# Query and key projections spread among the steps of neighbourhood attention, and its output accumulated in two PSUM banks instead of four

## The chip, the cores and the metric

The kernel runs on one core of a Trainium2 chip. A core has a matrix engine (TensorE, PE in the rows), a vector engine (VectorE, DVE), a scalar engine (ScalarE, ACT), GpSimd (POOL) and a sync engine (SyncE, SP), which issues nearly all transfers here. Each engine takes its instructions strictly in the order of its own program and waits on semaphores that the others raise. The metric is device time in microseconds for one execution, lower is better. Before the change three runs gave 3113.78, 3114.00 and 3114.54 us.

## What is computed

Two transformer blocks stand one behind the other, all in float32. The change lies in the second one, in its layer of neighbourhood attention: 512 tokens on a grid of 8 rows and 64 columns, 16 heads of 64, and 256 further context tokens to which every query attends. Cut to what matters:

```
q, k, v = jnp.split(a_lat @ w_qkv, 3, axis=-1)
qc, kc, vc = ... jnp.split(a_ctx @ w_qkv, 3, axis=-1)
s_lat = einsum('bnqhd,brnkhd->bhnqrk', q * scale, kb) + bias      # band of keys around the query
s_lat = where(col_ok, s_lat, NEG_INF)
s_ctx = einsum('bnqhd,bchd->bhnqc', qr, kc)
p = softmax(concatenate([s_lat, s_ctx], -1), -1)
o = einsum('bhnqrk,brnkhd->bnqhd', p_lat, vb) + einsum('bhnqc,bchd->bnqhd', p_ctx, vc)
o_lat @ w_out
```

Every large projection is made of three fp32r matmuls a product (`products`: high weights by low data, low weights by high data, high by high), whose sum stands in for one float32 product.

## The kernel before

`schedule()` writes one list of work items, and each engine's program walks that list and executes the items that concern it. So the place of an item in the list sets the order of its work on every engine at once, and an engine that must wait inside an item holds back all of its later items. Waits are only those on data and on buffers that must be free.

Weights come in blocks of 128 by 1024. SyncE loads them into a ring of three raw buffers (`NR`), ScalarE casts each into a high part (L1439, `t_whi`), and VectorE (even blocks, L1730) or GpSimd (odd blocks, L2157) subtracts to make the low part `t_wlo`. There are four slots for finished blocks (`NH`); `over` puts the `prep` item of block j+4 right behind the last matmul of block j. SyncE may load a block only when both parts of the block three before it are made.

`neighbourhood()` works in two halves of eight heads; a half has four pairs of heads (c) and each pair four blocks of 128 queries (b), 16 steps p = 4c + b. First the value rows of the half are made (`rows`, `rows_by_group`), SyncE copies shifted versions of them within the chip's memory (`na_shift`, L1151 and L1153, six transfers), the bias strips of the pair are loaded (`na_strip`, L1159, two transfers) and GpSimd subtracts them from the masks (`na_bias`, L2202, two instructions for each of three tables y). For one step the work goes

- `na_scores`: PE L1380 into banks 0 and 1 (one a head), drained by VectorE L2100, which adds the bias table of that kind of block and takes the row extremes; ScalarE L1680 exponentiates. Scores of p+1 need both banks drained.
- `na_probs` (one step later): VectorE L2108 and L2110 (TENSOR_SCALAR) scale the weights.
- `na_turn` (two steps later): PE L1391 transposes into banks 2 and 3, ScalarE L1686 copies out.
- `na_attend` (three steps later): PE L1407 multiplies with the values, into banks 4 and 5 for even pairs and 6 and 7 for odd ones.
- `na_y`: when a pair's four blocks are done, ScalarE L1693 and VectorE L2115 split its output into a high and a low part, head 0 at step 4c+7 and head 1 at step 4c+8.

Queries (`na_q`, 24 matmuls of 512 columns) and keys (`na_k`, 24 of 512 and 24 of 256) of pair c are projected by `q_and_k(c)` ahead of the scores of step p = c, so in the first four steps of each half. Steps 4 to 15 hold attention alone. Behind step 15 of half 0 the value rows of half 1 stand (two groups at steps 16 and 17, four after the last attend); behind step 15 of half 1 stands the output projection (`o_steps`, first in banks 0 and 1, then `na_o` on VectorE L2125).

Of the kernel before, what the change touches and what calls it, by code (L numbers as in the profile page):

```python
# [8 lines left out]
ALU = mybir.AluOpType  # L9
# [120 lines left out]
def schedule():  # L130
# [651 lines left out]
    def neighbourhood():  # L782
        pro = state["misc_free"]
        ov = {"q": pro, "k": pro, "v": pro}
        vslot = lambda tt: tt if tt < 4 else tt + 3
# [10 lines left out]
        o_specs = [(("na_o", j), (SLOT,), DC, ("yn",), [(0, "drain_dve", o_post(j))]) for j in range(DC)]  # L796
        o_steps = by_steps(o_specs[:4], SUB1, (0, 1))

# [5 lines left out]
        for half in range(2):  # L804
# [16 lines left out]

            def q_post(g, c, half=half):
                put("na_q", half=half, c=c, g=g.id, bank=g.bank, after=ov["q"])

            def k_post(g, c, half=half):
                put("na_k", half=half, c=c, g=g.id, bank=g.bank, t0=g.t0, n=g.n, after=ov["k"])

            def q_and_k(c, half=half):
                columns([(("na_qk", half * 4 + c), (SLOT,), DC, ("h", 6),
                          [(0, "drain_act", lambda g: q_post(g, c))])], SEG1, banks=(6, 7))  # L830
                last_h = columns([(("na_qk", 8 + half * 4 + c), (SLOT,), DC, ("h", 6),
                                   [(0, "drain_act", lambda g: k_post(g, c))])], SEG2, banks=(6, 7))
                state["h_free"] = [last_h]

# [28 lines left out]
            def attend(p, half=half):  # L863
                c, b = divmod(p, 4)
                to = [p % 2 * 2 + hd for hd in range(2)]
                banks = [4 + c % 2 * 2 + hd for hd in range(2)]
                before = [seat(banks[hd], "drain_dve", ("na_yh", half, c, hd)) if b == 0 else [] for hd in range(2)]
                put("na_attend", half=half, p=p, c=c, b=b, to=to, banks=banks, before=before,
                    tiles=(VSTART[BAND0[b]], VSTART[BAND0[b] + 128], 7, 8))
                for k in to:  # L870
                    turned_free[k] = [("na_ps", ("o", half, p))]

            strips(0)
            for y in range(3):
                bias(0, y)
            for p in range(16 + 3):
                if p < 4:
                    q_and_k(p)
                if p < 16:
                    c, b = divmod(p, 4)  # L880
                    scores(p)
# [12 lines left out]
                if p == 16 and half == 1:  # L894
                    closing()
                if p in (16, 17) and half == 0:
                    next(v_rows)
                if p >= 16 and half == 1:
                    next(o_steps), next(o_steps)
                if 0 <= p - 2 < 16:  # L900
                    turn_weights(p - 2)
                if p - 3 >= 0:
                    attend(p - 3)
                    for hd in range(2):
                        c, b = divmod(p - 4 - hd, 4)
# [262 lines left out]
def tensor_program(e, w, S, m, items):  # L1168
# [225 lines left out]
    def na_attend(it):  # L1394
# [4 lines left out]
        for kt in range(4):  # L1399
# [5 lines left out]
            for hd in range(2):  # L1405
                v = NVV + t * 512 + (it.c * 2 + hd) * 64
                done = e.matmul(m.PS[hd * 64:hd * 64 + 64, it.banks[hd], it.b * P:(it.b + 1) * P], m.at(v, 64),  # L1407
                                m.na_t(it.to[hd])[:, kt // 2, kt % 2 * P:(kt % 2 + 1) * P], start=kt == 0, stop=kt == 3,
# [13 lines left out]
def scalar_program(e, w, S, m, items, release):  # L1422
# [288 lines left out]
def vector_program(e, w, S, m, items, release):  # L1711
# [400 lines left out]
    def na_y(it):  # L2112
        k, pp = it.half * 4 + it.c, slice(it.hd * 64, it.hd * 64 + 64)
        w.wait_ge("na_act", ("y", k, it.hd))
        e.tensor_tensor(m.hid(1, k, 512, 0, L)[pp, :], m.PS[pp, it.bank, :], m.hid(0, k, 512, 0, L)[pp, :], ALU.subtract).then_inc(  # L2115
            *S["drain_dve"].of(("na_yh", it.half, it.c, it.hd), *([("na_y", it.half, it.c)] if it.hd else [])))

# [246 lines left out]
```

## Time and profile before

| what | value |
| --- | --- |
| median of three runs | 3114.0 us |
| the profiled execution | 3116.97 us |
| its span | 3115.2 us |
| PE busy | 2932.8 us, 94% of the span |
| PE weight loads (PEld) | 2476.5 us, 79% |
| DVE busy | 1508.3 us, 48% |
| ACT busy | 1049.0 us, 34% |
| POOL busy | 617.0 us, 20% |
| mean granted TensorE clock | 0.973 of full speed |

The profiled execution took 1.8 us more than its span, which counts from the first instruction to the last. A matmul's record outlasts the slot in which it is issued, so start-to-start distances tell what PE needs, and "idle" in a row understates a wait by a little.

### The profile page before, as it was taken

The numbers are of one execution on the slowest core, as the hardware profiler recorded it, in microseconds if no ns is written. First come the engines' busy times: TensorE is split into PE (matmuls) and PEld (weight loads), VectorE is DVE, ScalarE is ACT, GpSimd is POOL, SyncE is SP. The second block draws the span as 40 slices with busy tenths as digits, with TensorE's granted clock in tenths as the row PEclk, the third lists the DMA queues.
The fourth block names the chain that finished last, engine by engine and source line by source line (L and its number), as shares of the span: only waits on it lengthen the run. The fifth ranks groups of instructions, "written<-read, shape, count | busy, mean of one in ns | idle before, by whom it ended". The sixth has DMA issues, their size and how long they took to land.

```text
span 3115.2 us, 39771 instructions
## 1 busy us (share of the span) xinstructions
PE 2932.8 (94%) x15968; PEld 2476.5 (79%) x15968; DVE 1508.3 (48%) x2524; ACT 1049.0 (34%) x1814; POOL 617.0 (20%) x330
## 2 busy tenths in 40 slices
PE   7999977889999899999999799999998999899997
PEld 6888965678878886868687788888896777878887
DVE  4667575555766424233232835445555526532224
ACT  4322335543232532122222541122226535342222
POOL 2333212113323110101011011111102212112221
PEclk9999998889999999999999999999998999999999
DMA  3444321014444220102011023223312121122221
GB/s 136 166 147 164 115 76 54 27 55 163 151 155 141 76 75 34 61 14 82 27 68 41 28 67 124 88 82 122 115 55 88 57 68 45 55 76 100 96 100 55
DMA packets 84696, 268.80 MB, mean 86 GB/s; under 512 B 8992, under 2 KB 16544, under 8 KB 84128
## 3 DMA queue, kind: packets, MB, share of 16 engines
q1 hardware_dynamic: 84512, 266.25, 25.2%
q8 instruction: 127, 2.08, 0.3%
q14 instruction: 57, 0.47, 0.0%
HBM read 262.54 MB, written 2.10 MB: 85 GB/s over the span
## 4 chain that ended last, share of the span: by engine, by line
PE 82%; DVE 9%; ACT 5%; issue 2%; POOL 1%; DMA 1%; SPq 0%; DVEq 0%; ACTq 0%; POOLq 0%
PE ps L1170 25%; PE ps L1171 24%; PE ps L1172 24%; PE ps L1357 3%; PE ps L1348 1%; DVE t_misc L1820 1%; ACT t_whi L1439 1%; DVE t_misc L1750 1%; DVE t_wlo L1730 1%; PE ps L1380 1%; PE ps L1407 1%; POOL t_wlo L2157 1%; PE ps L1391 1%; PE ps L1260 1%; DVE t_x L1772 0%
## 5 line engine op out<-in xcount | busy, mean ns | idle before, releaser
L1170 PE MATMUL ps<-t_h,t_whi 128*128 128x512 f32 (+1 forms) x2736 | 975.5, 357 | 57.4 <-DVE t_wlo L1730 30.1
L1171 PE MATMUL ps<-t_h,t_wlo 128*128 128x512 f32 (+1 forms) x2736 | 968.2, 354 | 0.0
L1172 PE MATMUL ps<-t_h,t_whi 128*128 128x512 f32 (+1 forms) x2736 | 967.1, 353 | 0.0
L2157 POOL TENSOR_TENSOR t_wlo<-t_raw,t_whi 128x1024 fp32r<-128x1024 f32 (+3 forms) x201 | 485.9, 2417 | 2038.5 <-ACT t_whi L1439 2038.5
L1170 PEld LDWEIGHTS ps<-t_h,t_whi 128*128 128x128 f32 x2736 | 525.8, 192 | 133.1 <-issue 23.1
L1171 PEld LDWEIGHTS ps<-t_h,t_wlo 128*128 128x128 f32 x2736 | 526.0, 192 | 69.2 <-issue 1.0
L1172 PEld LDWEIGHTS ps<-t_h,t_whi 128*128 128x128 f32 x2736 | 525.1, 192 | 69.4
L1730 DVE TENSOR_TENSOR t_wlo<-t_raw,t_whi 128x1024 fp32r<-128x1024 f32 (+3 forms) x201 | 252.6, 1257 | 672.3 <-ACT t_whi L1439 672.0
L1170 PE MATMUL ps<-t_hid,t_whi 128*128 128x256 f32 (+1 forms) x1648 | 535.2, 325 | 16.8 <-DVE t_hid L1862 8.9
L1439 ACT CAST t_whi<-t_raw 128x1024 fp32r<-128x1024 f32 (+3 forms) x402 | 402.2, 1002 | 401.6 <-PE ps L1172 378.0
L1171 PE MATMUL ps<-t_hid,t_wlo 128*128 128x256 f32 (+1 forms) x1648 | 531.1, 322 | 0.0
L1172 PE MATMUL ps<-t_hid,t_whi 128*128 128x256 f32 (+1 forms) x1648 | 530.3, 322 | 0.0
L1170 PEld LDWEIGHTS ps<-t_hid,t_whi 128*128 128x128 f32 x1648 | 316.8, 192 | 44.4 <-DVE t_hid L1862 9.5
L1171 PEld LDWEIGHTS ps<-t_hid,t_wlo 128*128 128x128 f32 x1648 | 317.0, 192 | 23.0 <-issue 0.2
L1172 PEld LDWEIGHTS ps<-t_hid,t_whi 128*128 128x128 f32 x1648 | 316.6, 192 | 23.0
L1820 DVE CUSTOM_DVE_ANT_0 t_misc<-t_raw,t_misc 128x1024 f32<-128x1024 f32 x192 | 322.1, 1714 | 23.9 <-ACT t_misc L1431 16.5
L1515 ACT CAST t_hid<-t_tmp 128x512 fp32r<-128x512 f32 (+1 forms) x118 | 65.1, 552 | 381.8 <-DVE t_tmp L1859 381.8
L1859 DVE TENSOR_TENSOR t_tmp<-t_misc,ps 128x512 f32<-128x512 f32 (+1 forms) x118 | 70.6, 599 | 144.4 <-PE ps L1172 124.8
L1878 DVE SCALAR_TENSOR_TENSOR t_x<-ps,t_mod,t_x 128x256 f32<-128x256 f32 (+1 forms) x160 | 89.7, 574 | 78.1 <-PE ps L1172 78.0
L1170 PE MATMUL ps<-t_wlo,t_h 128*128 128x512 f32 x288 | 118.1, 410 | 6.3 <-DVE t_h L1811 3.1
L1862 DVE TENSOR_TENSOR t_hid<-t_tmp,t_hid 128x512 fp32r<-128x512 f32 (+1 forms) x118 | 84.9, 720 | 73.0 <-ACT t_hid L1515 73.0
L1171 PE MATMUL ps<-t_whi,t_h 128*128 128x512 f32 x288 | 114.9, 399 | 0.0
(225 smaller groups left out, 2467.0 us busy)
## 6 DMA issues: line engine op xcount, KB each, us to landing
t_raw<-in_gu SPq DMA_DIRECT2D x176, 512.0 KB, 3.2
t_raw<-in_ada SPq DMA_DIRECT2D x96, 512.0 KB, 3.3
t_raw<-in_dn SPq DMA_DIRECT2D x48, 448.0 KB, 3.3
t_raw<-in_dn SPq DMA_DIRECT2D x28, 512.0 KB, 3.6
t_raw<-in_ret_v SPq DMA_DIRECT2D x16, 512.0 KB, 3.2
t_raw<-in_ret_qk SPq DMA_DIRECT2D x16, 512.0 KB, 3.2
t_raw<-in_ret_g SPq DMA_DIRECT2D x16, 512.0 KB, 3.2
t_raw<-in_ret_o SPq DMA_DIRECT2D x16, 512.0 KB, 3.6
```

The source lines that it names most:

```text
L1170: e.matmul(out, whi, xlo, start=first, stop=False, skip_group_check=shared)
L1171: e.matmul(out, wlo, xhi, start=False, stop=False, skip_group_check=shared)
L1172: return e.matmul(out, whi, xhi, start=False, stop=last, skip_group_check=shared)
L1357: done = e.matmul(m.PS[:, c, 0:it.n], m.at(RVV + it.kt * 512 + c * P, P), pw, start=it.i == 0, stop=it.last)
L1439: e.copy(m.WHI[:, j % NH, 0:n], m.RAW[:, it.raw % NR, 0:n]).then_inc(*S["hi"].of(j))
L1515: e.copy(m.hid(0, it.k, it.pitch, it.t0, it.n), m.tmp(it.off, it.n)).then_inc(*S["hid_hi"].of(it.los[0]))
L1730: e.tensor_tensor(m.WLO[:, j % NH, 0:n], m.RAW[:, it.raw % NR, 0:n], m.WHI[:, j % NH, 0:n], ALU.subtract).then_inc(*S["lo_dve"].of(j))
L1820: e.tensor_tensor_reduce(m.at(ADA_OUT + who * 1024, 1024), m.RAW[:, it.raw % NR, :], m.cond(who), 1.0, 0.0, ALU.mult, ALU.add, m.mod(it.la ...
L1859: e.tensor_tensor(t, s, m.ps(it), ALU.mult).then_inc(*S["drain_dve"].of(it.g, ("up", it.f, *it.los[0][1:3], it.t0)))
L1862: e.tensor_tensor(m.hid(1, it.k, it.pitch, it.t0, it.n), t, m.hid(0, it.k, it.pitch, it.t0, it.n), ALU.subtract).then_inc(*S["hid_lo"].of( ...
L1878: e.scalar_tensor_tensor(out=x, in0=m.ps(it), scalar=m.mod(it.layer, it.who, it.gm, it.j), in1=x, op0=ALU.mult, op1=ALU.add).then_inc(*S[" ...
L2157: e.tensor_tensor(m.WLO[:, j % NH, 0:n], m.RAW[:, it.raw % NR, 0:n], m.WHI[:, j % NH, 0:n], ALU.subtract).then_inc(*S["lo_pool"].of(j))
```

## The change

The projections of pair n+1 (pairs counted 0 to 7 across both halves) now stand inside the attention steps of pair n: its queries at b = 1, its keys at b = 2, after that step's attend. Only pair 0 is projected ahead of its half; pair 4, the first of half 1, is projected during steps 13 and 14 of half 0, so that half 1 begins with scores. All pairs accumulate their output in banks 4 and 5. `na_y` is one item for both heads, at b = 2 of the next pair, ahead of the keys. The output projection begins at step 14 of half 1 in banks 6 and 7, with two of its steps there and one in each later step. The weight blocks are used in the new order (pair 4's ahead of the values of half 1). The arithmetic is the same. The core of the diff:

```diff
-            def q_and_k(c, half=half):
-                columns([(("na_qk", half * 4 + c), (SLOT,), DC, ("h", 6),
-                          [(0, "drain_act", lambda g: q_post(g, c))])], SEG1, banks=(6, 7))
...
+            def queries(pair):
+                half, c = divmod(pair, 4)
+                after = [("na_ps", ("s", 0, c * 4 + 3, 1))] if half else pro
...
             def attend(p, half=half):
                 c, b = divmod(p, 4)
                 to = [p % 2 * 2 + hd for hd in range(2)]
-                banks = [4 + c % 2 * 2 + hd for hd in range(2)]
-                before = [seat(banks[hd], "drain_dve", ("na_yh", half, c, hd)) if b == 0 else [] for hd in range(2)]
+                before = [seat(4 + hd, "drain_dve", ("na_yh", half, c, hd)) if b == 0 else [] for hd in range(2)]
...
+            if half == 0:
+                queries(0)
+                keys(0)
             for p in range(16 + 3):
-                if p < 4:
-                    q_and_k(p)
+                c, b = divmod(p, 4)
                 if p < 16:
-                    c, b = divmod(p, 4)
                     scores(p)
...
-                if p == 16 and half == 1:
-                    closing()
...
-                if p >= 16 and half == 1:
-                    next(o_steps), next(o_steps)
...
                 if p - 3 >= 0:
                     attend(p - 3)
-                    for hd in range(2):
-                        c, b = divmod(p - 4 - hd, 4)
-                        if 0 <= c < 3 and b == 3:
-                            put("na_y", half=half, c=c, hd=hd, bank=4 + c % 2 * 2 + hd, over=state["hid_free"])
-            for hd in range(2):
-                put("na_y", half=half, c=3, hd=hd, bank=6 + hd, over=state["hid_free"])
-            ov["q"] = ov["k"] = [("na_ps", ("s", half, 15, 1))]
+                    if b == 2:
+                        put("na_y", half=half, c=c - 1, over=state["hid_free"])
+                if p < 16 and half * 4 + c < 7:
+                    if b == 1:
+                        queries(half * 4 + c + 1)
+                    if b == 2:
+                        keys(half * 4 + c + 1)
+                elif half == 1:
+                    if p == 14:
+                        closing()
+                        next(o_steps)
+                    if p >= 14:
+                        next(o_steps)
```

The first place is PE's program at the start of half 0. Before, where L1380 is the scores of step 0 and L1170 to L1172 are the projection on either side of it:

```order
L1171 MATMUL ps<-t_h,t_wlo 128x256
L1172 MATMUL ps<-t_h,t_whi 128x256
L1380 MATMUL ps<-t_misc 128x256 x4
L1170 MATMUL ps<-t_h,t_whi 128x512
L1171 MATMUL ps<-t_h,t_wlo 128x512
```

Now, with every line number one higher:

```order
L1172 MATMUL ps<-t_h,t_wlo 128x256
L1173 MATMUL ps<-t_h,t_whi 128x256
L1381 MATMUL ps<-t_misc 128x256 x8
L1171 MATMUL ps<-t_h,t_whi 128x512
L1172 MATMUL ps<-t_h,t_wlo 128x512
```

The scores of steps 0 and 1 now stand directly one behind the other, with no projection between them.

The second place is ScalarE's program in half 0 around steps 6 to 9. Before (L1680 the exponential of a step, L1686 the copy of turned weights, L1693 the high part of the pair's output):

```order
L1686 COPY t_x<-ps 128x2x256 x2
L1680 ACTIVATE t_tmp,t_misc<-t_tmp,t_misc 128x512 x2
L1686 COPY t_x<-ps 128x2x256 x2
L1693 CAST t_hid<-ps 64x512
L1680 ACTIVATE t_misc<-t_misc 128x512 x2
L1686 COPY t_x<-ps 128x2x256 x2
L1693 CAST t_hid<-ps 64x512
```

Now (L1669 copies the next pair's queries, L1674 its keys, L1440 casts a weight block, L1696 is the high part of the output):

```order
L1687 COPY t_x<-ps 128x2x256 x2
L1669 ACTIVATE t_misc<-ps 128x512
L1440 CAST t_whi<-t_raw 128x1024
L1681 ACTIVATE t_tmp,t_misc<-t_tmp,t_misc 128x512 x2
L1687 COPY t_x<-ps 128x2x256 x2
L1696 CAST t_hid<-ps 64x512 x2
L1674 COPY t_misc<-ps 128x512
```

The two casts of the pair's output have moved together and stand in the step whose end is the projection of keys.

The third place is ScalarE's program between the halves. Before (L1526 copies value rows, L1668 the queries and L1673 the keys of pair 4):

```order
L1693 CAST t_hid<-ps 64x512 x2
L1526 COPY t_misc<-ps 128x512 x5
L1439 CAST t_whi<-t_raw 128x1024 x4
L1526 COPY t_misc<-ps 128x512
L1668 ACTIVATE t_misc<-ps 128x512
L1439 CAST t_whi<-t_raw 128x1024
L1673 COPY t_misc<-ps 128x512
L1673 COPY t_misc<-ps 128x256
L1439 CAST t_whi<-t_raw 128x1024
L1680 ACTIVATE t_misc<-t_misc 128x512 x2
```

Now:

```order
L1696 CAST t_hid<-ps 64x512 x2
L1527 COPY t_misc<-ps 128x512 x5
L1440 CAST t_whi<-t_raw 128x1024 x4
L1527 COPY t_misc<-ps 128x512
L1681 ACTIVATE t_misc<-t_misc 128x512 x2
L1681 ACTIVATE t_tmp,t_misc<-t_tmp,t_misc 128x512 x2
L1669 ACTIVATE t_misc<-ps 128x512
```

Pair 4's queries and keys are gone from between the last copy of value rows and the first exponentials of half 1. The order of SyncE's transfers up to the strips of pair 4 is the same as before.

## Rows read from the trace of the kernel before

**Rows 1.** The page: busy time of each engine, chain that ended last.

```profile
PE 2932.8 (94%) x15968; PEld 2476.5 (79%) x15968; DVE 1508.3 (48%) x2524; ACT 1049.0 (34%) x1814; POOL 617.0 (20%) x330
...
PE 82%; DVE 9%; ACT 5%; issue 2%; POOL 1%; DMA 1%; SPq 0%; DVEq 0%; ACTq 0%; POOLq 0%
```

**Rows 2.** Timeline of PE, scores: start, duration, line, [idle before, releaser].

```profile
2455.50 1.13 PE L1380 MATMUL ps<-t_misc 64*128 64x256 f32 x8
...
2465.43 1.14 PE L1380 MATMUL ps<-t_misc 64*128 64x256 f32 x8
...
2468.55 1.14 PE L1380 MATMUL ps<-t_misc 64*128 64x256 f32 x8
...
2471.66 1.13 PE L1380 MATMUL ps<-t_misc 64*128 64x256 f32 x8
...
2480.05 1.13 PE L1380 MATMUL ps<-t_misc 64*128 64x256 f32 x8 [1.03 <-DVE t_misc L2100]
...
2498.79 1.13 PE L1380 MATMUL ps<-t_misc 64*128 64x256 f32 x8
...
2602.75 1.13 PE L1380 MATMUL ps<-t_misc 64*128 64x256 f32 x8
...
2646.05 1.13 PE L1380 MATMUL ps<-t_misc 64*128 64x256 f32 x8
```

**Rows 3.** Timeline of ACT and DVE behind step 8's scores (2471.66).

```profile
2472.82 0.58 ACT L1693 CAST t_hid<-ps 64x512 fp32r<-64x512 f32 x1
2473.43 0.68 DVE L2115 TENSOR_TENSOR t_hid<-ps,t_hid 64x512 fp32r<-64x512 f32 x1 [0.64 <-ACT t_hid L1693]
...
2474.04 0.67 DVE L2100 CUSTOM_DVE_ANT_1 t_tmp<-ps,t_misc 128x512 f32<-128x512 f32 x1
```

**Rows 4.** Timeline of POOL and DVE behind the last keys of half 0.

```profile
2457.07 2.37 POOL L2157 TENSOR_TENSOR t_wlo<-t_raw,t_whi 128x1024 fp32r<-128x1024 f32 x1 [13.46 <-ACT t_whi L1439]
...
2458.09 1.63 DVE L2110 TENSOR_SCALAR t_tmp<-t_tmp,t_misc 128x512 f32<-128x512 f32 x1
```

**Rows 5.** Timeline of the first scores of half 0 and their drains.

```profile
2409.51 1.13 PE L1380 MATMUL ps<-t_misc 64*128 64x256 f32 x8 [0.56 <-ACT t_misc L1673]
2410.57 0.50 PE L1170 MATMUL ps<-t_h,t_whi 128*128 128x512 f32 x1
...
2411.26 0.69 DVE L2100 CUSTOM_DVE_ANT_1 t_misc<-ps,t_misc 128x512 f32<-128x512 f32 x1
```

**Rows 6.** Timeline between the halves, PE, SP and POOL.

```profile
2542.07 0.39 PE L1172 MATMUL ps<-t_whi,t_h 128*128 128x512 f32 x1
2542.30 0.39 PE L1170 MATMUL ps<-t_h,t_whi 128*128 128x512 f32 x1
...
2548.73 1.07 SPq L1159 DMA_DIRECT2D t_misc<-in_rpb  x2
...
2555.05 4.20 POOL L2202 TENSOR_TENSOR t_misc<-t_misc 128x256 f32<-128x256 f32 x6 [7.43 <-DMA t_misc<-in_rpb]
...
2556.76 1.13 PE L1380 MATMUL ps<-t_misc 64*128 64x256 f32 x8 [0.56 <-ACT t_misc L1673]
```

**Rows 7.** Timeline of PE, the first two matmuls of a run of value rows.

```profile
2501.91 0.50 PE L1170 MATMUL ps<-t_wlo,t_h 128*128 128x512 f32 x1
2502.24 0.40 PE L1171 MATMUL ps<-t_whi,t_h 128*128 128x512 f32 x1
```

**Rows 8.** PE by 2 us: stretch, its length, busy (instructions), granted clock, DMA.

```profile
2718.00:2720.00 2.00, 2.00 (x11) 0.50 0.04 8
2720.00:2722.00 2.00, 2.00 (x15) 0.78 0.00 0
```

**Rows 9.** Timeline of PE behind attention: output projection, resume in the next stage.

```profile
2665.36 0.38 PE L1170 MATMUL ps<-t_hid,t_whi 128*128 128x256 f32 x1 [0.49 <-DVE t_hid L2115]
...
2668.66 0.36 PE L1170 MATMUL ps<-t_hid,t_whi 128*128 128x256 f32 x1 [1.24 <-DVE t_misc L2125]
...
2717.58 0.58 PE L1170 MATMUL ps<-t_h,t_whi 128*128 128x256 f32 x1 [2.86 <-DVE t_h L1811]
```

More of the change, by code:

```diff
@@ L783, in neighbourhood @@
         pro = state["misc_free"]
-        ov = {"q": pro, "k": pro, "v": pro}
+        ov = {"v": pro}
         vslot = lambda tt: tt if tt < 4 else tt + 3
@@ L796, in neighbourhood @@
         o_specs = [(("na_o", j), (SLOT,), DC, ("yn",), [(0, "drain_dve", o_post(j))]) for j in range(DC)]
-        o_steps = by_steps(o_specs[:4], SUB1, (0, 1))
+        o_steps = by_steps(o_specs[:4], SUB1, (6, 7))
         def closing():
@@ L820, in neighbourhood, with keys @@
             put("na_shift", half=half, after=ov["v"])
[L822 to L826, printed above, removed]
-            def q_and_k(c, half=half):
-                columns([(("na_qk", half * 4 + c), (SLOT,), DC, ("h", 6),
-                          [(0, "drain_act", lambda g: q_post(g, c))])], SEG1, banks=(6, 7))
-                last_h = columns([(("na_qk", 8 + half * 4 + c), (SLOT,), DC, ("h", 6),
-                                   [(0, "drain_act", lambda g: k_post(g, c))])], SEG2, banks=(6, 7))
-                state["h_free"] = [last_h]
+            def queries(pair):
+                half, c = divmod(pair, 4)
+                after = [("na_ps", ("s", 0, c * 4 + 3, 1))] if half else pro
+                post = lambda g: put("na_q", half=half, c=c, g=g.id, bank=g.bank, after=after)
+                columns([(("na_qk", pair), (SLOT,), DC, ("h", 6), [(0, "drain_act", post)])], SEG1, banks=(6, 7))
+            def keys(pair):
+                half, c = divmod(pair, 4)
+                after = [("na_ps", ("s", 0, c * 4 + 3, 1))] if half else pro
+                post = lambda g: put("na_k", half=half, c=c, g=g.id, bank=g.bank, t0=g.t0, n=g.n, after=after)
+                state["h_free"] = [columns([(("na_qk", 8 + pair), (SLOT,), DC, ("h", 6), [(0, "drain_act", post)])], SEG2, banks=(6, 7))]
             def strips(c, half=half):
@@ L865, in attend @@
                 to = [p % 2 * 2 + hd for hd in range(2)]
-                banks = [4 + c % 2 * 2 + hd for hd in range(2)]
-                before = [seat(banks[hd], "drain_dve", ("na_yh", half, c, hd)) if b == 0 else [] for hd in range(2)]
-                put("na_attend", half=half, p=p, c=c, b=b, to=to, banks=banks, before=before,
+                before = [seat(4 + hd, "drain_dve", ("na_yh", half, c, hd)) if b == 0 else [] for hd in range(2)]
+                put("na_attend", half=half, p=p, c=c, b=b, to=to, before=before,
                     tiles=(VSTART[BAND0[b]], VSTART[BAND0[b] + 128], 7, 8))
@@ L1406, in na_attend @@
                 v = NVV + t * 512 + (it.c * 2 + hd) * 64
-                done = e.matmul(m.PS[hd * 64:hd * 64 + 64, it.banks[hd], it.b * P:(it.b + 1) * P], m.at(v, 64),
+                done = e.matmul(m.PS[hd * 64:hd * 64 + 64, 4 + hd, it.b * P:(it.b + 1) * P], m.at(v, 64),
                                 m.na_t(it.to[hd])[:, kt // 2, kt % 2 * P:(kt % 2 + 1) * P], start=kt == 0, stop=kt == 3,
@@ L1689, in na_y @@
     def na_y(it):
-        k, pp = it.half * 4 + it.c, slice(it.hd * 64, it.hd * 64 + 64)
+        k = it.half * 4 + it.c
         w.wait_ge("na_ps", ("o", it.half, it.c * 4 + 3))
         wait_all(it.over)
-        e.copy(m.hid(0, k, 512, 0, L)[pp, :], m.PS[pp, it.bank, :]).then_inc(*S["na_act"].of(("y", k, it.hd)))
+        for hd in range(2):
+            pp = slice(hd * 64, hd * 64 + 64)
+            e.copy(m.hid(0, k, 512, 0, L)[pp, :], m.PS[pp, 4 + hd, :]).then_inc(*S["na_act"].of(("y", k, hd)))
     def move_x(it):
@@ L2112, in na_y @@
     def na_y(it):
[L2113 to L2116, printed above, removed]
+        k = it.half * 4 + it.c
+        for hd in range(2):
+            pp = slice(hd * 64, hd * 64 + 64)
+            w.wait_ge("na_act", ("y", k, hd))
+            e.tensor_tensor(m.hid(1, k, 512, 0, L)[pp, :], m.PS[pp, 4 + hd, :], m.hid(0, k, 512, 0, L)[pp, :], ALU.subtract).then_inc(
+                *S["drain_dve"].of(("na_yh", it.half, it.c, hd), *([("na_y", it.half, it.c)] if hd else [])))
     def na_o(it):
```

## The prediction

> **What bounds the kernel now.** I read the page first: PE is busy 94% of the span, and the chain of work that ended last lies on PE for 82%, the rest mostly where PE waits for VectorE or ScalarE [rows 1]. PE's matmuls stay the same, so the change can only take away or add waits of PE, in the attention stage from 2409 to 2670 us. There I read PE's timeline by the starts of the scores. In a step that holds attention alone, scores, turned weights and attend follow one another without a wait, and a step takes 3.11 us (2468.55 to 2471.66 [rows 2]). From step 3 (2455.50) to step 15 (2498.79) of half 0, twelve steps take 43.29 us where 12 x 3.11 = 37.32 would do: 5.97 us of waiting. Half 1 shows the same, 43.30 us from 2602.75 to 2646.05 [rows 2].
>
> Two things make these waits. **First**, `na_y`: behind the scores of step 8 ScalarE casts head 0 of pair 0 at 2472.82, VectorE waits for it and subtracts from 2473.43, and only then, at 2474.04, begins to drain the scores of step 8 [rows 3], which had ended at about 2472.8 [rows 2]. The scores of step 9 come 0.7 us late by this. Head 1 does it again one step later: step 10 starts at 2480.05 after 1.03 us of idle PE, released by VectorE's drain [rows 2]. Pair 1 repeats both. **Second**, the first bare steps behind a projection: from 2455.50 to 2465.43 three steps take 9.93 us instead of 9.33, so 0.6 us are lost [rows 2]. There GpSimd makes the low part of an odd block (2.37 us from 2457.07), and VectorE's TENSOR_SCALAR beside it takes 1.63 us and ends just behind it [rows 4].
>
> **The change part by part.** The sum is against the profiled execution (3116.97 us, 1.8 more than its span). The median of the runs is 3.0 us less, and I put the same difference on it.
>
> *a. `na_y` under the keys.* Both heads now lie ahead of a keys projection: two casts of 0.58 and two subtractions of 0.68 us [rows 3] behind an attend, with some 8.4 us of matmuls over them (24 of 512 columns at 0.23 us from start to start [rows 6], and 24 of 256, which I take at half of that, 0.12). Banks 4 and 5 are wanted again by the attend of the next step, behind those matmuls: two banks are enough, at no cost. For pair 6 the cover is two output steps, the next scores and the turned weights (2 x 1.44 + 1.06 + 1.0, so 5 us) against 2.5. If the cover were gone, the price would be up to the whole chain, 2 x (0.58 + 0.68) = 2.5 us for each pair. The 5.97 us of both halves fall away: **-11.9 us**.
>
> *b. The entry loss comes oftener.* In each half keys stand at steps 2, 6 and 10 with bare steps behind, each with its odd block on GpSimd (the parity of the blocks stays). Three entries of 0.6 us [rows 2, 4] per half: 6 x 0.6 = **+3.6 us**. Behind the keys of step 14 of half 0 one bare step and then value rows follow, which hide it. Bounds: 0 if the TENSOR_SCALAR falls clear of GpSimd, 1.3 each if it always loses as much as the worst step of [rows 2] shows (a 1.03 us idle and its tail).
>
> The Trainium skill (SBUF — State Buffer, "Who interferes with whom") says that the port pair which VectorE and GpSimd share is locked for a whole instruction and that the other fully blocks. By it a TENSOR_SCALAR that comes right behind the start of the GpSimd subtraction would wait out nearly all of its 2.37 us; by the row the step loses 0.6, and I take the row.
>
> *c. Scores 0 and 1 adjacent, half 0.* Scores 0 start at 2409.51 and PE is free again at 2410.57; VectorE's second drain ends at 2411.26 + 0.69 = 2411.95 [rows 5]. Scores 1 need both banks, and nothing stands between now: about **+1.4 us**. Not less than 1.2; 3.0 if an instruction like the 1.63 us one of [rows 4] gets ahead on VectorE.
>
> *d. Half 1 begins without its projection.* This is the large term. Value rows end at 2542.30, where pair 4's queries start now [rows 6]. SyncE cannot issue the bias strips of pair 4 before three weight loads and six shifts: it issues them at 2548.73, they land at 2555.05, GpSimd's six subtractions take 4.20 us, so 0.70 each, and the scores came at 2556.76, just in time: the 14 us of projection hid this whole chain [rows 6]. SyncE's and GpSimd's orders here are unchanged and hang on the end of the value rows (the weight loads wait for slots freed there), not on the projection. Now scores 0 run at 2542.30 to 2543.36. VectorE cannot drain them before the tables of both heads: 2555.05 + 1.40 = 2556.45, plus 0.69 of draining = 2557.14. PE is strictly in order, so scores 1, and behind them the queries of pair 5, stand until 2557.2: **+13.9 us**. The adjacent-scores wait of (c) is in it. The old wait for the keys' copy there (0.56 us of idle and the tail of a matmul [rows 6]) goes: **-0.7 us**. The strips were 6.3 us under way with all DMA queued ahead of them; 5 us would make it 12.6, one more transfer ahead 15.4.
>
> *e. The clock.* After such a gap PE resumes at the lower of its two levels. In the next stage PE resumes at 2717.58 [rows 9] at a granted clock of 0.50, and the stretch from 2720 has 0.78, full again at about 2720.9 [rows 8]: 3.3 us at 1.2 instead of 2.4 GHz lose half of that, **+1.65 us** (0 to 2.5).
>
> *f. More runs of matmuls.* The first matmul behind other work takes 0.33 us to the next [rows 7] against 0.23 within a run (2542.07 to 2542.30 [rows 6]), and a little more on the second: 0.12 a run. I count 22 runs instead of 13: **+1.1 us**.
>
> *g. The end.* Behind the last attend two output steps (12 matmuls of 0.12, 1.44 us each) now stand ahead of the one that needs pair 7's output, instead of one, so the idle 0.49 us goes; and the second token half no longer waits for bank 0, since the first sits in banks 6 and 7, so the 1.24 us go [rows 9]. With the 0.16 us by which a matmul's record outlasts its slot (0.39 against 0.23 [rows 6]) at each: **-2.0 us** (-0.6 if something else holds it).
>
> Sum: -11.9 + 3.6 + 1.4 + 13.9 - 0.7 + 1.65 + 1.1 - 2.0 = **+7.0 us**. The profiled execution would take 3124.0 and the median 3121.0 us. Half 0 alone gains about 2 us, half 1 loses 9.
>
> **The rivals.**
>
> *The strips are in time (faster).* If the wait in (d) did not come, because the tables are ready when PE reaches the scores, only the 1.4 us of (c) stand there: 7.0 - 13.9 + 1.4 - 1.65 = -7.2, so 3106.8 us. For it speaks only that VectorE, GpSimd and ScalarE are nearly idle there. Against it: the first table waited for a DMA until 2555.05 [rows 6], and nothing ahead of that transfer is removed. It decides if the strips land before about 2548. 8%.
>
> *The wait is half as long (no change).* If the shifts and strips get through while fewer weight loads compete, and the tables are there at about 2549, PE loses 7 us less: 3114 us. The two weight loads and two strips issued behind pair 4's strips may have slowed these. Against it: they are behind it in the same queue. 8%.
>
> *The port costs more (slower).* If at each of the six entries the TENSOR_SCALAR meets GpSimd's 2.37 us from their start, six times 1.8 us (2.37 less 0.6 [rows 4]) more come: 3131.8 us; half of that, or a second fall of the clock, 3126. 10%. The rule of the Trainium skill (SBUF — State Buffer, "Who interferes with whom") speaks for it.
>
> **How the numbers follow.** My forecast has 74%, its own range from the bounds is 3117 to 3125. This kernel's runs lie within 0.03%, and I take 0.2%, 6.2 us, as what a measurement can tell from no change: 3120.2 us is the border to slower, and my 3121.0 lies just over it. Of the 74 I give 46 to slower and 28 to no change; with the rivals: faster 8, same 36, slower 56. The range of 3112 to 3127 takes in the forecast, the shorter wait and the milder half of the port; it leaves out the faster rival and the dearest port case.
>
> **What the profile would show.** (a) L2115's successor only under keys, no PE idle released by VectorE's drain at steps 9, 10, 13, 14. (b) a step of about 3.6 us behind each keys projection. (c) 1.4 us of PE idle between the first two scores. (d) one PE gap of 13 to 15 us near 2540, whose end is a drain that waits for GpSimd's tables, which wait for the strips' DMA. (e) a clock of 0.50 behind it for 3 us. (g) no gap between the output steps. It would be wrong if the gap in (d) is far from 14 us, if the clock falls elsewhere in the stage, or if the bare steps keep waiting for reasons other than `na_y`.

## The result, and the profile after

The changed kernel takes **3127.3 us** (median of 6 runs, 3124.5 to 3128.8). The kernel before, run beside it, took 3114.3 (3113.8 to 3118.4). The ratio is 1.0039, 95% interval 1.0026 to 1.0052: slower by more than 0.2%. The forecast was 3121.0, a ratio of 1.0022. As an absolute time the result lies 0.3 us above the range of 3112 to 3127; the ratio of 1.0039 on the 3114.0 us of before is 3126.1, inside it. In a second group of runs on one chip (11 and 24 runs), the ratio was 1.0026 (1.0017 to 1.0035). The profiled execution took 3125.55 us (span 3123.8), 8.6 more than that of before; my sum said 7.0 more.

PE is as busy as before, as the page's lines on engines and on the chain show (compare [rows 1]):

```profile
PE 2937.1 (94%) x15968; PEld 2476.3 (79%) x15968; DVE 1505.5 (48%) x2524; ACT 1048.1 (34%) x1814; POOL 617.1 (20%) x330
PE 80%; DVE 10%; ACT 4%; issue 3%; POOL 1%; DMA 1%; SPq 0%; DVEq 0%; ACTq 0%; POOLq 0%
```

For every kernel I read three numbers from the profile. The **stage** runs from the first scores to the first matmul of the next stage's mean: 2409.51 to 2698.18 before (288.7 us), 2409.23 to 2707.01 after (297.8). The **idle** is the sum of PE's waits in it and of the one right before the first scores (0.55 to 0.56 us in every kernel). The **clock cost** is the sum, over windows of 1 us, of PE's busy time times (1 - granted clock). Before it was 1.7 us, after 5.4. The stage less the clock cost is 287.0 before and 292.4 after: 5.4 us of waits and starts.

PE's timeline after, in a pair of half 0, from step 3 (2430.57) to the next queries (2440.49), as [rows 2]:

```profile
2430.57 1.14 PE L1381 MATMUL ps<-t_misc 64*128 64x256 f32 x8
2433.68 1.14 PE L1381 MATMUL ps<-t_misc 64*128 64x256 f32 x8
2435.71 0.66 PE L1392 MATMUL ps<-t_con,t_tmp 128*128 128x128 f32 x4 [0.21 <-DVE t_tmp L2113]
2437.32 1.13 PE L1381 MATMUL ps<-t_misc 64*128 64x256 f32 x8
2440.49 0.50 PE L1171 MATMUL ps<-t_h,t_whi 128*128 128x512 f32 x1
```

Three steps take 9.92 us, 0.59 over 9.33, and every pair repeats it. The idle of 0.6 and 1.0 us that VectorE's late drains made [rows 2] is gone from the whole stage. What is there instead, on the same engine's timeline (head of half 0, value rows between the halves, head of half 1, behind the last attend of half 1):

```profile
2411.82 1.99 PE L1381 MATMUL ps<-t_misc 64*128 64x256 f32 x8 [1.46 <-DVE t_misc L2103]
...
2533.95 0.50 PE L1171 MATMUL ps<-t_wlo,t_h 128*128 128x512 f32 x1 [2.37 <-ACT t_misc L1527]
...
2557.53 1.14 PE L1381 MATMUL ps<-t_misc 64*128 64x256 f32 x8
2571.81 2.08 PE L1381 MATMUL ps<-t_misc 64*128 64x256 f32 x8 [13.14 <-DVE t_misc L2103]
...
2673.24 1.09 PE L1408 MATMUL ps<-t_x,t_misc 128*64 128x128 f32 x16
2674.26 0.39 PE L1171 MATMUL ps<-t_hid,t_whi 128*128 128x256 f32 x1
```

The large one is 13.14 us between scores 0 and 1 of half 1. It is the least stable of them: 12.8 to 14.0 us in the five profiles that keep this part of the change; what sets the difference is open. Its cause, on the timelines of DVE, POOL and SP's queue (compare [rows 6]):

```profile
2557.49 2.14 DVE L1733 TENSOR_TENSOR t_wlo<-t_raw,t_whi 128x1024 fp32r<-128x1024 f32 x1 [1.50 <-ACT t_whi L1440]
2570.28 0.69 DVE L2103 CUSTOM_DVE_ANT_1 t_misc<-ps,t_misc 128x512 f32<-128x512 f32 x1 [10.65 <-POOL t_misc L2207]
...
2556.17 2.38 POOL L2162 TENSOR_TENSOR t_wlo<-t_raw,t_whi 128x1024 fp32r<-128x1024 f32 x1 [39.93 <-ACT t_whi L1440]
2560.46 2.34 POOL L2162 TENSOR_TENSOR t_wlo<-t_raw,t_whi 128x1024 fp32r<-128x1024 f32 x1 [1.91 <-ACT t_whi L1440]
2569.42 4.14 POOL L2207 TENSOR_TENSOR t_misc<-t_misc 128x256 f32<-128x256 f32 x6 [6.62 <-DMA t_misc<-in_rpb]
...
2563.85 2.04 SPq L1160 DMA_DIRECT2D t_misc<-in_rpb  x4
```

The strips are issued 6.3 us behind the end of the value rows, GpSimd gets the first at 2569.42, VectorE drains from 2570.28. That is step (d) as it was foretold. The clock is the second finding. Windows of 1 us at the head of half 0 (window, its length, busy us and instructions of PE, PEld, DVE, ACT and POOL, then PE's granted clock and the DMA share and GB/s):

```profile
2411.00:2412.00 1.00, 0.18 (x2) 0.21 (x4) 0.67 (x4) 0.99 (x3) 1.00 (x1) 0.98 0.00 0
2412.00:2413.00 1.00, 1.00 (x6) 0.94 (x7) 0.00 (x0) 0.86 (x4) 1.00 (x2) 0.50 0.00 0
2414.00:2415.00 1.00, 1.00 (x3) 0.81 (x4) 1.00 (x3) 0.48 (x1) 0.00 (x0) 0.50 0.97 373
2416.00:2417.00 1.00, 1.00 (x6) 0.84 (x5) 0.28 (x1) 0.04 (x1) 0.00 (x0) 1.00 0.00 0
```

Behind 1.46 us of idle the granted clock fell to 0.50 (1.2 GHz) for 3.4 us, and eight scores took 1.99 instead of 1.13 us. It fell for 3.4 us behind the 2.37 us at 2533.95 too, where the kernel before has the same idle and kept its clock; its own fall came at 2683.

### The profile page after: what moved, and what is told of

Its sections match the earlier page's. It is cut to its first block, busy times and chain, and to the rows that moved or that the text cites. A ratio compares the mean times of both kernels' runs of the same rounds, so it can differ in the third digit from the quotient of the medians.

```text
span 3123.8 us, 39774 instructions
## 1 busy us (share of the span) xinstructions
PE 2937.1 (94%) x15968; PEld 2476.3 (79%) x15968; DVE 1505.5 (48%) x2524; ACT 1048.1 (34%) x1814; POOL 617.1 (20%) x330
## 4 chain that ended last, share of the span: by engine, by line
PE 80%; DVE 10%; ACT 4%; issue 3%; POOL 1%; DMA 1%; SPq 0%; DVEq 0%; ACTq 0%; POOLq 0%
PE ps L1171 24%; PE ps L1172 24%; PE ps L1173 24%; PE ps L1358 3%; DVE t_misc L1823 2%; ACT t_whi L1440 1%; PE ps L1349 1%; DVE t_wlo L1733 1%; PE ps L1381 1%; PE ps L1408 1%; DVE t_misc L1753 1%; POOL t_wlo L2162 1%; PE ps L1392 1%; DMA t_x<-in_ctx 1%; PE ps L1261 1%
## 5 line engine op out<-in xcount | busy, mean ns | idle before, releaser
L1172 PE MATMUL ps<-t_h,t_wlo 128*128 128x512 f32 (+1 forms) x2736 | 969.1, 354 | 0.0
L1172 PEld LDWEIGHTS ps<-t_h,t_wlo 128*128 128x128 f32 x2736 | 526.5, 192 | 69.0 <-issue 1.0
L1171 PE MATMUL ps<-t_hid,t_whi 128*128 128x256 f32 (+1 forms) x1648 | 535.0, 325 | 14.9 <-DVE t_hid L1865 8.7
L1440 ACT CAST t_whi<-t_raw 128x1024 fp32r<-128x1024 f32 (+3 forms) x402 | 402.0, 1002 | 400.7 <-PE ps L1173 377.1
L1172 PE MATMUL ps<-t_hid,t_wlo 128*128 128x256 f32 (+1 forms) x1648 | 530.9, 322 | 0.0
L1172 PEld LDWEIGHTS ps<-t_hid,t_wlo 128*128 128x128 f32 x1648 | 316.7, 192 | 23.0 <-issue 0.2
L1172 PE MATMUL ps<-t_whi,t_h 128*128 128x512 f32 x288 | 114.5, 398 | 0.0
```

The costliest lines, as they stand in the source:

```text
L1171: e.matmul(out, whi, xlo, start=first, stop=False, skip_group_check=shared)
L1172: e.matmul(out, wlo, xhi, start=False, stop=False, skip_group_check=shared)
L1440: e.copy(m.WHI[:, j % NH, 0:n], m.RAW[:, it.raw % NR, 0:n]).then_inc(*S["hi"].of(j))
```

## The experiments

Ten further kernels, and the changed one again; all changes are to the changed kernel. Stage, clock cost and idle are of one profile each (the two profiles of the changed kernel differ by 0.3 us in the stage less clock); ratios are to the kernel before in the same group.

| kernel | stage | clock cost | stage less it | PE idle in the stage | ratio (95%) |
|---|---|---|---|---|---|
| before | 288.7 | 1.7 | 287.0 | 17.2 | |
| changed | 297.8 | 5.4 | 292.4 | 20.9 | 1.0039 (1.0026 to 1.0052) |
| changed, again | 296.2 | 3.5 | 292.7 | 21.1 | 1.0026 (1.0017 to 1.0035) |
| pair 4 back | 285.4 | 3.2 | 282.2 | 11.0 | 0.9987 (0.9978 to 0.9995) |
| tables early | 286.8 | 5.1 | 281.7 | 10.3 | 0.9996 (0.9987 to 1.0005) |
| strips alone early | 289.5 | 3.5 | 286.1 | 14.4 | one run |
| tables early, queries behind step 0 | 296.7 | 4.8 | 291.9 | 19.9 | 1.0027 (1.0016 to 1.0039) |
| end as before | 303.7 | 6.4 | 297.3 | 25.8 | 1.0059 (1.0046 to 1.0073) |
| copy back uncovered | 302.9 | 1.6 | 301.4 | 30.3 | one run |
| low parts on VectorE | 303.9 | 5.0 | 298.9 | 28.9 | one run |
| two banks alone | 285.5 | 1.7 | 283.8 | 14.6 | 0.9987 (0.9978 to 0.9996) |
| pair 4 back, first pair dense | 283.4 | 1.7 | 281.7 | 10.0 | 0.9984 (0.9974 to 0.9993) |
| tables early, first pair dense | 282.0 | 1.7 | 280.3 | 8.3 | 0.9976 (0.9966 to 0.9986) |

**The changed kernel again.**

> The changed kernel itself once more, beside the others of this group on one chip. Theory (the stage is 9.1 us longer, and the rest of a run's time varies by some us with where the clock falls): ratio to the kernel before 1.003 with these bounds around it, stage (first scores to the first mean matmul) 297.8 within 2 us, and the part ahead of it and behind it as in the kernel before within 3 us. Rival (the change moves something outside of the stage too): the part ahead or behind differs by 3 us or more from the kernel before in this profile again, in the same direction.

The stage is 296.2 us with the same idles (1.46, 2.37, 13.28, 2.17). Ahead of it lie 2410.1 us (2409.5 before), behind it 419.1 (417.0 before, 416.8 in the first profile of the changed kernel). Nothing outside moves in one direction. This time the clock stayed full behind the same 1.46 us:

```profile
2412.72 1.13 PE L1381 MATMUL ps<-t_misc 64*128 64x256 f32 x8 [1.46 <-DVE t_misc L2103]
```

So the fall there is not the change's alone; it comes in some executions. Without the clock the two profiles give 292.4 and 292.7.

**Pair 4's projections back ahead of half 1.**

```diff
-            if half == 0:
-                queries(0)
-                keys(0)
+            queries(half * 4)
+            keys(half * 4)
...
-                if p < 16 and half * 4 + c < 7:
+                if p < 16 and half * 4 + c < 7 and (half, c) != (0, 3):
```

> The changed kernel with one part undone: pair 4's queries and keys stand ahead of half 1 again, not in steps 13 and 14 of half 0. Theory (the wait for pair 4's bias tables was uncovered, everything else as I summed it): the 13.14 us of PE idle behind scores 0 of half 1 fall to 1.4 (scores 0 and 1 stay adjacent), the 2.0 us of lower clock behind it go, the old wait for the keys' copy (0.7) comes back: -11.7 - 2.0 + 0.7 = -13.0, so about 3114 us. Rival (the cost lies in the two banks or in the many short runs of projection in the steps, not in the cross-half part): the time stays above 3122. Rival (the tables come late in any case, because weights of later pairs are loaded earlier now): the idle only moves behind the projection, 3 us or more of it stay, above 3117.

The stage falls by 12.4 us (10.2 without the clock), and the 13.14 us are 1.46:

```profile
2498.61 1.09 PE L1407 MATMUL ps<-t_x,t_misc 128*64 128x128 f32 x16 [1.16 <-DVE t_hid L2119]
...
2558.50 1.88 PE L1380 MATMUL ps<-t_misc 64*128 64x256 f32 x8 [1.46 <-DVE t_misc L2102]
```

One part undone turns 0.3 to 0.4% slower into 0.13% faster. Both rivals fall: the total is no longer above the kernel before, and no wait of 3 us is left. The first row is new: pair 2's copy back lost its cover with the keys of step 14, and the attend waits 1.16 us for its bank.

**Pair 4's tables early, and its strips alone.** The first kernel issues the strips in step 12 of half 0 and makes the tables in steps 13, 15 and 16; the second does only the first of the two.

```diff
-            strips(0)
-            for y in range(3):
-                bias(0, y)
             if half == 0:
+                strips(0)
+                for y in range(3):
+                    bias(0, y)
...
+                if half == 0 and p == 12:
+                    strips(0, 1)
+                if half == 0 and p in (13, 15, 16):
+                    bias(0, (13, 15, 16).index(p), 1)
```

> The changed kernel with pair 4's two bias strips issued in step 12 of half 0 and its six tables made in steps 13, 15 and 16, in place of the head of half 1. Theory (the half boundary waits for the strips' DMA and nothing else): scores 0 and 1 of half 1 start 1.1 + 1.4 us apart instead of 14.3, the low clock behind the long gap goes (2.0): -11.7 - 2.0 = -13.7, so about 3113.6; if the clock falls behind the short gap too, as it did at the head of half 0, 1.7 of it come back, 3115. Rival (shifts, value rows' copies or pair 4's own keys are late as well): a second wait takes the place, the two starts stay over 5 us apart, 3119 or more.

> The changed kernel with only the two bias strips of pair 4 issued early, in step 12 of half 0; GpSimd makes the six tables at the head of half 1 as before. Theory (the DMA alone is late, since GpSimd idles there): the tables are made while value rows run, scores 1 follow scores 0 after 2.6 to 3.6 us as where the tables were early too. Rival (GpSimd's order holds the tables back, behind an odd block's low part or a wait for freed tables): the two starts lie 6 us or more apart.

With the tables early, the wait falls from 13.14 to 2.46 us, 1.0 more than the 1.4 of the theory, and the stage by 11.0 us. PE, DVE and POOL there:

```profile
2559.76 1.13 PE L1385 MATMUL ps<-t_misc 64*128 64x256 f32 x8 [2.46 <-DVE t_misc L2107]
...
2556.13 2.14 DVE L1737 TENSOR_TENSOR t_wlo<-t_raw,t_whi 128x1024 fp32r<-128x1024 f32 x1 [1.50 <-ACT t_whi L1444]
2558.30 0.69 DVE L2107 CUSTOM_DVE_ANT_1 t_misc<-ps,t_misc 128x512 f32<-128x512 f32 x1
...
2554.81 2.38 POOL L2166 TENSOR_TENSOR t_wlo<-t_raw,t_whi 128x1024 fp32r<-128x1024 f32 x1 [36.47 <-ACT t_whi L1444]
```

VectorE's second low part here takes 2.14 us, where one that meets nothing takes 1.23: it starts beside GpSimd's and ends at 2558.27, 1.08 behind the end of GpSimd's, as if it had begun there. The drain of scores 0 stands behind it. With the strips alone early, the wait is 6.64 us, and here the rival held:

```profile
2566.29 2.08 PE L1384 MATMUL ps<-t_misc 64*128 64x256 f32 x8 [6.64 <-DVE t_misc L2106]
...
2561.60 2.34 POOL L2165 TENSOR_TENSOR t_wlo<-t_raw,t_whi 128x1024 fp32r<-128x1024 f32 x1 [2.07 <-ACT t_whi L1443]
2563.90 4.14 POOL L2210 TENSOR_TENSOR t_misc<-t_misc 128x256 f32<-128x256 f32 x6
```

The strips had long landed, but GpSimd works in order, and the low parts of two odd blocks, whose weights are ready only around the end of the value rows, stand ahead of the tables. So, undone in this order, the 13.14 us divide: 6.5 are the strips' DMA, 4.2 GpSimd's order, 1.0 VectorE's slow low part, and 1.46 are the adjacent scores. What lies between these kernels is one profile each, so a share is good to some tenths of a us, that of the DMA to about one.

**Queries behind step 0, with the tables early.**

```diff
-                    if b == 1:
+                    if b == 0:
                         queries(half * 4 + c + 1)
```

> As the run with the tables made early, and in each pair the queries of the next stand behind step 0 instead of step 1, keys behind step 2 as they were. Theory: scores 0 and 1 are no longer adjacent in either half, which gives back 1.45 us of idle twice and 1.7 us of low clock at the head of half 0; the entry loss of 0.6 stays where GpSimd's block falls in the bare step 3, and VectorE's own block (some 1.1 us) now falls in the bare step 1, which can cost up to 0.6 each, five times: between 3.0 and 4.6 us less than the run with the tables early, about 3110, 4 us below the kernel before. Rival (bare steps need to stand in a row, each projection behind which one begins costs an entry): six more entries of 0.6, so only 1 us less.

Both theories were wrong: the stage is 9.9 us longer than with the tables early alone. PE waits 3.20 us at scores 2 of each half and 1.15 us at the scores of steps 6, 10 and (in half 0) 14:

```profile
2416.97 2.08 PE L1385 MATMUL ps<-t_misc 64*128 64x256 f32 x8 [3.20 <-DVE t_misc L2107]
...
2445.74 1.13 PE L1385 MATMUL ps<-t_misc 64*128 64x256 f32 x8 [1.15 <-DVE t_misc L2107]
2447.14 1.11 PE L1396 MATMUL ps<-t_con,t_tmp 128*128 128x128 f32 x8 [0.27 <-ACT t_x L1691]
...
2443.14 1.22 DVE L1737 TENSOR_TENSOR t_wlo<-t_raw,t_whi 128x1024 fp32r<-128x1024 f32 x1 [5.96 <-ACT t_whi L1444]
2444.29 0.68 DVE L2107 CUSTOM_DVE_ANT_1 t_tmp<-ps,t_misc 128x512 f32<-128x512 f32 x1
```

VectorE's low part of the next block can start only when ScalarE has cast it, and that follows the slot that the queries free. The drain of the next scores stands behind it. In the changed kernel the keys cover this; here nothing does. A pair takes 28.78 us from its step 3 to the next one's, against 27.24.

**The low parts of the stage's odd blocks on VectorE** (blocks 311 to 329 are the stage's).

```diff
-    return "lo_pool" if j % 2 else "lo_dve"
+    return "lo_pool" if j % 2 and not 311 <= j <= 329 else "lo_dve"
...
-        if j % 2 == 0:
+        if j % 2 == 0 or 311 <= j <= 329:
...
-        if j % 2 == 1:
+        if j % 2 == 1 and not 311 <= j <= 329:
```

> The changed kernel with the low parts of all this stage's weight blocks on VectorE, the odd ones too. Theory (the entry loss of 0.6 is TENSOR_SCALAR held up beside GpSimd's block; VectorE's own block takes 1.23 us of its time instead): no TENSOR_SCALAR over 0.5 us in steps 3 and 4 of a pair, but about 1.15 + 0.27 us of idle at the scores behind, as where VectorE's block fell in a bare step, so the entry is 1.2 to 1.4 long instead of 0.5 to 0.6: +4 to +5 us in the stage. Rival (the entry loss has nothing to do with GpSimd and comes from the order of ScalarE's work behind a projection): TENSOR_SCALAR still shows 1.6 us once for each entry, or the loss stays 0.5 to 0.6 though it shows 0.49.

The stage less clock grows by 6.5 us, a little over the forecast: PE's idle at step 4 of a pair is 0.94 to 1.06 and 0.28, scores 1 of half 0 come 1.3 us later yet. The longest TENSOR_SCALAR is 1.08 us, where the changed kernel has 1.63 once a pair. So the rival falls, but "none over 0.5" did not hold either: those of 1.06 to 1.08 us stand beside GpSimd's tables. First this run, then the changed kernel:

```profile
2436.88 1.06 DVE L2113 TENSOR_SCALAR t_tmp<-t_tmp,t_misc 128x512 f32<-128x512 f32 x1
...
2436.23 1.42 POOL L2207 TENSOR_TENSOR t_misc<-t_misc 128x256 f32<-128x256 f32 x2 [8.49 <-DVE t_misc L2103]
```

```profile
2433.16 1.63 DVE L2113 TENSOR_SCALAR t_tmp<-t_tmp,t_misc 128x512 f32<-128x512 f32 x1
2434.70 0.15 DVE L2111 RECIPROCAL t_misc<-t_misc 128x1 f32<-128x1 f32 x1
...
2432.14 2.36 POOL L2162 TENSOR_TENSOR t_wlo<-t_raw,t_whi 128x1024 fp32r<-128x1024 f32 x1 [18.25 <-ACT t_whi L1440]
```

The row of 1.63 us starts 1.02 us into GpSimd's instruction and ends 0.29 behind its end, at 2434.50; that of 1.06 also ends 0.29 behind the end of GpSimd's second table, at 2437.65. With 2556.13 above, these are two kinds of VectorE instruction that wait out most of GpSimd's. This agrees with the whole-instruction lock of the Trainium skill (SBUF — State Buffer, "Who interferes with whom"). The loss for PE at step 4 is still 0.53 us (3.64 instead of 3.11) and not 1.14; the difference would be slack of VectorE in that step, which no run isolates.

**The copy back uncovered.** `na_y` is put behind the keys, ahead of the next scores.

```diff
+                if b == 3 and p > 3:
+                    put("na_y", half=half, c=c - 1, over=state["hid_free"])
                 if p < 16:
                     scores(p)
...
-                    if b == 2:
+                    if p == 18:
                         put("na_y", half=half, c=c - 1, over=state["hid_free"])
```

> The changed kernel with the copy back of attended values put behind the keys' projection, ahead of the drain of the next step's scores, instead of under it; banks and all else as changed. Theory (its cover is the projection): the chain of two casts and two subtractions (1.19 + 1.41, overlapping to about 1.9) now stands ahead of that drain; the next scores come 0.8 to 1.5 us late for each of six pairs and the next attend may wait too: +5 to +9 us in the stage. Rival (VectorE and ScalarE have room in that step anyway): under 2 us in all.

The stage less clock grows by 8.9 us, at the upper end of the forecast; 0.9 of it stands at the head of half 1, where this profile has 14.00 us of idle for 13.14, so some 8 are the copy's. PE waits 1.33, 0.25 and 0.42 us for each of the pairs with bare steps behind, and a pair's two steps take 8.45 instead of 6.75.

```profile
2457.31 1.09 PE L1410 MATMUL ps<-t_x,t_misc 128*64 128x128 f32 x16 [1.33 <-DVE t_hid L2122]
2458.66 1.13 PE L1383 MATMUL ps<-t_misc 64*128 64x256 f32 x8 [0.25 <-DVE t_misc L2105]
2460.21 1.12 PE L1394 MATMUL ps<-t_con,t_misc 128*128 128x128 f32 x8 [0.42 <-ACT t_x L1689]
```

**Two banks alone**, with the projections ahead of steps 0 to 3 as before.

```diff
-            if half == 0:
-                queries(0)
-                keys(0)
...
+                if p < 4:
+                    queries(half * 4 + p)
+                    keys(half * 4 + p)
...
-                if p < 16 and half * 4 + c < 7:
-                    if b == 1:
-                        queries(half * 4 + c + 1)
-                    if b == 2:
-                        keys(half * 4 + c + 1)
-                elif half == 1:
+                if half == 1:
```

> One part alone: all projections stand ahead of steps 0 to 3 of each half as in the kernel before; attended values go back in two banks (both heads in one piece behind the pair's last attend, with nothing but attention over it) and the end is the changed kernel's. Theory (uncovered, one piece costs PE 1.17 us for each pair, as at step 15 of the run with pair 4 back, where the kernel before lost 2.98 for a pair in two pieces): six pairs make 7.0 instead of the 11.9 us of waits of before, and the end gives 2.05: stage 288.7 - 4.9 - 2.05 = 281.7 us, 0.2% under the kernel before. Rival (the banks are wanted by the next attend, so the whole chain of 2.5 us shows): stage 288.7 + 3 - 2 = 290.

The stage is 285.5, not 281.7: 3.2 us under the kernel before. The direction was right, the price of one piece was not:

```profile
2477.32 1.09 PE L1403 MATMUL ps<-t_x,t_misc 128*64 128x128 f32 x16 [1.16 <-DVE t_hid L2115]
2478.66 1.13 PE L1376 MATMUL ps<-t_misc 64*128 64x256 f32 x8 [0.25 <-DVE t_misc L2098]
2480.22 1.11 PE L1387 MATMUL ps<-t_con,t_misc 128*128 128x128 f32 x8 [0.42 <-ACT t_x L1682]
```

Besides the 1.16 us at the attend there are 0.25 at the scores and 0.42 at the turned weights, and the tails of the matmuls: the scores of step 8 start 4.66 us behind those of step 7 and those of step 9 another 3.63, so 2.07 over two bare steps. Two pieces cost 2.68 (12.01 us from step 8 to step 11 before, where 9.33 would do); the 2.98 of the expectation is half of the 5.97 and has half of an entry's 0.6 in it. Pairs 0, 1, 4 and 5 so gain 2.4 us, pair 2 loses 1.25 behind step 15, and the end gives 2.0. The ratio is that of pair 4 back: the spreading of the projections there takes another 1.6 us off the stage less clock, too little for the ratios to tell.

**The end as before.**

```diff
-        o_steps = by_steps(o_specs[:4], SUB1, (6, 7))
+        o_steps = by_steps(o_specs[:4], SUB1, (0, 1))
...
-                    if p == 14:
+                    if p == 16:
                         closing()
-                        next(o_steps)
-                    if p >= 14:
-                        next(o_steps)
+                    if p >= 16:
+                        next(o_steps), next(o_steps)
```

> The changed kernel with the output projection's first blocks begun as before: banks 0 and 1, behind the last scores, two steps at a time. Theory: the 0.49 us behind the last attend and the 1.24 us for bank 0 come back, with the tails 2.05 us: 3129.3. Rival (these waits were shadows of na_y under the old places): no idle of PE behind the output steps but the 2.16 us that the changed kernel has, 3127.

It costs 4.9 us without the clock, not 2.05. Of these, 0.6 stand at the head of half 1 (13.76 us of idle), so the end costs some 4.3:

```profile
2661.71 1.09 PE L1407 MATMUL ps<-t_x,t_misc 128*64 128x128 f32 x16 [1.17 <-DVE t_hid L2119]
2664.61 1.94 PE L1391 MATMUL ps<-t_con,t_tmp 128*128 128x128 f32 x8 [1.80 <-ACT t_x L1686]
```

The wait for bank 0 (1.24) is back; the 0.49 is not. The output steps had also been pair 6's cover, and without them its copy back costs 1.17 at the attend and 1.80 behind it.

**Two versions with the first pair dense** (the second pair's queries behind step 0 and its keys behind step 1), one on pair 4 back, one on the tables early.

```diff
-                    if b == 1:
+                    if b == (1 if c else 0):
                         queries(half * 4 + c + 1)
-                    if b == 2:
+                    if b == (2 if c else 1):
                         keys(half * 4 + c + 1)
```

> The run with pair 4's projections back ahead of half 1, and for the first pair of each half the next pair's queries stand behind step 0 and keys behind step 1, as in the kernel before; later pairs keep steps 1 and 2. Theory: the 1.46 us between scores 0 and 1 go in both halves, and one fall of the clock (1.7): stage 285.4 - 2.9 - 1.7 = 280.8 us, total 5 us under that run, 0.25% under the kernel before. Rival (as where all queries stood behind step 0: VectorE's low part of the even block, 1.23 us, runs ahead of the drain of scores 1, and the next scores wait): 1 to 3 us of idle come at scores 2, the stage stays above 283.

> The run with pair 4's tables made early, and queries and keys of the second pair of each half behind steps 0 and 1. Theory: the 1.46 us at the head of half 0 and the 2.46 at that of half 1 go, with up to two falls of the clock (1.7 each): stage 286.8 - 3.9 - 3.4 = 279.5 us, 0.3% under the kernel before. Rival (what made the 2.46, VectorE's low part taking 2.14 instead of 1.23 us beside GpSimd's, only moves on to scores 2): the stage stays above 284.

Both waits behind scores 0 go, but PE now waits for VectorE at the scores of step 3 of each half (0.47 us) and at the turned weights behind them (0.51), so about 1.2 us goes for each 1.46 gained: from scores 0 to scores 6 of half 0 it takes 35.03 us instead of 35.34. The stages are 283.4 and 282.0, 2 to 3 us over the forecast. The second has the lowest ratio of the study, 0.9976, some 7 us under the kernel before by it (the medians of the group, 3113.8 and 3118.6, are 4.8 apart); its interval overlaps that of the first.

## Why the prediction was right, and where it was off

The class (slower by over 0.2%) and the main mechanism, a wait of 14 us at the head of half 1 for pair 4's tables, held. By its steps:

- **(a)** Right. The idle behind `na_y` is gone in both halves (10.7 of the 11.9 us; the other 1.2 are the two entries of before, which (b) counts anew). The cover is real: without it the stage loses some 8 us.
- **(b)** Right: 0.59 us an entry against 0.6. That GpSimd's odd block makes it is supported, not isolated: taking the block off GpSimd takes the 1.63 us row away, but puts 1.2 us of work on VectorE.
- **(c)** Right: 1.46 against 1.4. The fall of the clock behind it in the first profile, 1.7 us, was not in the sum.
- **(d)** Right in size: 14.28 us from scores 0 to scores 1, 14.9 foretold; undoing this part gave back 10.2 us and 2.2 of clock. The chain was incomplete. I wrote that the strips' DMA decides; strips in time leave 6.64 us, because GpSimd's odd blocks stand ahead of the tables. The upper bound of 15.4 us, for one more transfer, had no row behind it. My rival of 3106.8 held that strips in time would be enough; strips in time did not bring the tables in time. Where the tables were, the stage less clock came 5.3 us under the kernel before, and the ratio was 0.9996.
- **(e)** 2.0 against 1.65 behind the long gap (PE busy 4.0 us at 1.2 GHz). But this was one fall of three: with 1.7 at the head of half 0 and 1.7 at the value rows, less the fall of 2683 that the kernel before had, the clock costs 3.7 us more, not 1.65 (1.8 more in the second profile, where the head of half 0 kept its clock). A fall elsewhere in the stage was one of my signs of being wrong, and it came: the price of a fall was near, that there would be only one was wrong.
- **(f)** Not measured by itself. (a) to (d) and (g) by what the rows show give -11.9 + 3.5 + 1.5 + 13.1 - 0.7 - 2.1 = +3.4; the stage without clock grew by 5.4. What is left is 2.0, against 1.1 for this term.
- **(g)** Right: no idle between 2673.24 and the next wait, which the kernel before has too, and with two banks alone the end gave 2.0 us. Undone, it costs twice that, and only the 1.24 us come back as I had them; the rest is pair 6's copy back, for which these output steps are the cover, as (a) said.

The sum was 1.6 us low against the profile (8.6); the clock alone was 2.0 low. That (f) was 0.9 low and (d) 0.8 high, and that the rest of the program took 0.5 less, evened out by luck. **The step that failed is the one that turned the profile into a median**: "the median of the runs is 3.0 us less, and I put the same difference on it". It rested on 3 runs within 0.03%. Beside the experiments the kernel before took 3113.7 to 3124.5 us, and the time goes with the mean clock of the run: in one group 3114.2 to 3118.4 at 0.973, 3116.5 to 3120.9 at 0.972, 3118.8 to 3122.1 at 0.971. Each thousandth is some 3 us. The profile of before lay 3.0 above its median, that of the changed kernel 1.7 below, and this makes the other 4.7 of the 6.3 us. In the three later groups the kernel before has medians of 3117.5 to 3119.1, so the first three runs were low, rather than the profile high. My 3121.0 lay 0.8 us over my border to slower; that the class came out clear is more than the sum could promise. As a ratio the forecast (1.0022) lies inside the interval of the larger group (1.0017 to 1.0035) and just below that of the first.

## What to carry to other kernels

Before a projection (or any filler) is moved away, list everything that it covers on every in-order engine: here one block of matmuls hid a DMA, GpSimd's queue and VectorE's low part, and taking away the first alone left half of the wait. Where a low-rate helper is triggered by a freed slot, put it so that its burst falls under long matmuls; one step's difference cost 1.5 us a pair. Judge a change of 0.2% by ratios to runs beside it, and take the granted clock out of each profile before you compare sums.

## What the hardware showed that was not expected

- The granted clock fell to 0.50 (1.2 GHz) for 3.4 us behind quite short idles, and not each time: behind the 1.46 us between adjacent scores in 2 of 8 cases, behind the 2.37 us at the value rows in 8 of 13 profiles, behind the 2.16 us in the output projection in 6 of 13. The same kernel did both in two executions. With 3.4 us of busy PE each costs 1.7 us. A handful of these would make the spread from run to run; the times go with the mean clock, but single falls were seen in the profiles alone.
- VectorE's TENSOR_TENSOR took 2.14 instead of 1.23 us, its TENSOR_SCALAR 1.63 instead of 0.49, when they met GpSimd's; both ended a little behind the end of GpSimd's instruction (1.08 and 0.29 us). The drains of the scores, which read a PSUM bank and a table, did not stretch: all 64 in the stage of the changed kernel take 0.68 or 0.69 us, that of 2435.57 beside six tables of GpSimd too:

```profile
2435.57 0.68 DVE L2103 CUSTOM_DVE_ANT_1 t_tmp<-ps,t_misc 128x512 f32<-128x512 f32 x1
...
2434.46 4.89 POOL L2207 TENSOR_TENSOR t_misc<-t_misc 128x256 f32<-128x256 f32 x6
```
